# A two-layer conformer and attention trunk: the input and the parameters laid out by the host as columns, statistics and taps at other blocks

## What is computed

```python
def rms_norm(x, g):
    y = xf * lax.rsqrt(jnp.mean(xf * xf, axis=-1, keepdims=True) + RMS_EPS)
    return y.astype(x.dtype) * g

def conformer_conv(x, w_in, b_in, dw, dw_b, ln_g, ln_b, w_out, b_out):
    h = x @ w_in + b_in                 # 2048 -> 4096
    a, gate = jnp.split(h, 2, axis=-1)
    h = a * jax.nn.sigmoid(gate)
    h = causal_dwconv(h, dw, dw_b)      # 31 taps over the tokens
    h = jax.nn.silu(layer_norm(h, ln_g, ln_b))
    return h @ w_out + b_out

# in reference(): h = rms_norm(x, norm_mix[0]); x = x + conformer_conv(h, ...)
```

## Time and profile before

| what | us |
|---|---|
| median of 3 runs | 2141.56 |
| lowest and highest | 2141.47, 2142.43 |
| the profiled execution, its time | 2142.64 |
| its span, first to last instruction | 2140.8 |
| TensorE busy in it | 2125.7 |

### The profile page before, as it was taken

One profiled execution on the slowest core, in us unless ns is written; L12 is line 12 of the kernel. 1 busy time (PEld: TensorE's weight loads), 2 busy tenths in 40 slices (PEclk: granted clock), 3 DMA queues, 4 the chain that ended last, 5 costly groups with the idle time before them and its releaser, 6 DMA issues.

```text
span 2140.8 us, 30475 instructions
## 1 busy us (share of the span) xinstructions
PE 2125.7 (99%) x11011; PEld 1812.3 (85%) x11011; DVE 1452.6 (68%) x2137; ACT 1056.8 (49%) x1501; POOL 45.7 (2%) x50
## 2 busy tenths in 40 slices
PE   9999999999999999999999999999999999999998
PEld 7788788888888888888888888888888888888887
DVE  6766757777777774454688867667777777764444
ACT  7554655544445443444554444554544445444443
POOL 5300000000000000000000000000000000000000
PEclk9999999999999999999999999999999999999999
DMA  8555456666666655555656554566666666656553
GB/s 309 175 186 191 138 178 183 190 191 183 194 184 189 191 185 189 193 190 191 191 163 176 181 175 155 191 182 183 190 190 184 194 183 189 192 190 215 195 195 114
DMA packets 513820, 399.07 MB, mean 186 GB/s; under 512 B 6558, under 2 KB 425848, under 8 KB 513408
## 3 DMA queue, kind: packets, MB, share of 16 engines
q1 hardware_dynamic: 513568, 397.96, 60.0%
q10 hardware_dynamic: 192, 0.28, 0.0%
HBM read 396.11 MB, written 2.10 MB: 186 GB/s over the span
## 4 chain that ended last, share of the span: by engine, by line
PE 95%; DVE 2%; DMA 1%; ACT 1%; SPq 0%; issue 0%; DVEq 0%; ACTq 0%
PE acc L1520 35%; PE acc L1525 18%; PE acc L1554 12%; PE acc L1555 12%; PE acc L1556 12%; PE acc L1826 1%; PE acc L1825 1%; PE acc L1824 1%; DMA sb_stage<-in_conv_w_in 1%; DVE sb_w_lo L918 1%; PE aux L1595 0%; PE aux L1835 0%; ACT sb_w_hi L564 0%; PE aux L1783 0%; PE aux L1664 0%
## 5 line engine op out<-in xcount | busy, mean ns | idle before, releaser
L918 DVE TENSOR_TENSOR sb_w_lo<-sb_stage,sb_w_hi 128x1024 fp32r<-128x1024 f32 (+1 forms) x743 | 904.9, 1221 | 516.8 <-ACT sb_w_hi L564 513.4
L564 ACT ACTIVATE sb_w_hi<-sb_stage 128x1024 fp32r<-128x1024 f32 (+1 forms) x743 | 780.4, 1053 | 657.4 <-PE acc L1556 373.9
L1520 PE MATMUL acc<-sb_normed,sb_w_hi 128*128 128x512 f32 x3264 | 1027.6, 396 | 0.0
L1525 PEld LDWEIGHTS acc<-sb_normed,sb_w_lo 128*128 128x128 f32 x3264 | 613.2, 188 | 144.8
L1525 PE MATMUL acc<-sb_normed,sb_w_lo 128*128 128x256 f32 x3264 | 641.4, 278 | 0.0
L1520 PEld LDWEIGHTS acc<-sb_normed,sb_w_hi 128*128 128x128 f32 x3264 | 497.7, 189 | 0.6
L1554 PE MATMUL acc<-sb_w_hi,sb_hidden 128*128 128x512 f32 x674 | 262.5, 389 | 0.0
L1556 PE MATMUL acc<-sb_w_hi,sb_hidden 128*128 128x512 f32 x674 | 262.3, 389 | 0.0
L1555 PE MATMUL acc<-sb_w_lo,sb_hidden 128*128 128x512 f32 x674 | 262.3, 389 | 0.0
L576 ACT ACTIVATE sb_corr<-acc 128x256 f32<-128x256 f32 x204 | 76.8, 376 | 210.8 <-PE acc L1525 210.7
L1556 PEld LDWEIGHTS acc<-sb_w_hi,sb_hidden 128*128 128x128 f32 x674 | 126.5, 188 | 26.4
(11 more groups left out here) (221 smaller groups left out, 1645.1 us busy)
## 6 DMA issues: line engine op xcount, KB each, us to landing
sb_stage<-in_ffn_w_gate SPq DMA_DIRECT2D x86, 1024.0 KB, 5.4
sb_stage<-in_ffn_w_up SPq DMA_DIRECT2D x86, 1024.0 KB, 5.5
sb_stage<-in_ffn_w_down SPq DMA_DIRECT2D x80, 1024.0 KB, 5.0
sb_stage<-in_attn_w_qkv SPq DMA_DIRECT2D x48, 1024.0 KB, 5.3
sb_stage<-in_conv_w_in SPq DMA_DIRECT2D x30, 1024.0 KB, 5.6
sb_stage<-in_conv_w_out SPq DMA_DIRECT2D x16, 1024.0 KB, 5.1
sb_stage<-in_attn_w_o SPq DMA_DIRECT2D x16, 1024.0 KB, 5.0
sb_stage<-in_ffn_w_down SPq DMA_DIRECT2D x8, 768.0 KB, 4.4
```

The lines of the kernel that those rows point to most:

```text
L564: nc.scalar.activation(w_hi[:, (2 * first + h) % PIECES, 0:size], stage[:, first % STAGES, off:off + size], ACT.Copy).then_inc(hi_ready, 1)
L918: nc.vector.tensor_tensor(w_lo[:, slot, 0:size], stage[:, first % STAGES, off:off + size], w_hi[:, slot, 0:size].bitcast(F32), ALU.subtrac ...
L1520: nc.tensor.matmul(acc[:, bank, :], w_hi[:, slot, q * P:(q + 1) * P], operand[:, k, :], start=begin, stop=False, skip_group_check=True)
L1525: return nc.tensor.matmul(acc[:, bank, T:2 * T], w_lo[:, slot, q * P:(q + 1) * P], operand[:, k, 0:T], start=False, stop=end, skip_group_c ...
```

## The change

The host hands in x a second time, as columns (`x_cols`: feature on the partition, tile, token), and the parameter vectors as columns. x_cols is loaded into `x_t`, which lies over `conv` (free at that time), and ScalarE and VectorE read it in SBUF. The transposes of x, `turn_params`, its row buffers and `keep_params`' copies are gone; 13 filler matmuls (`keep_clock`) stand where 6 stood. `resid`, still needed for the squares and the residual, is loaded in two pieces of 1 MB after block 4's weights. Other steps move: the squares from turns 2 and 3 to 3 and 4, the first gate to turn 5, the row scale to turn 5, the table's split from turn 7 to 6, and in turns 4 and 5 both halves are split ahead of the small steps.

```diff
+        x_t = conv[:, :, :].rearrange("p b d -> p (b d)").rearrange("p (k t) -> p k t", t=T)
...
-                return sp.dma_start(resid[:, :, begin:end], x_in[0].rearrange("(b p) d -> p b d", p=P)[:, :, begin:end])
-            width = D // X_PARTS
-            load_x(0, 2 * P).then_inc(x_first, 16)
+                return sp.dma_start(x_t[:, begin:end, :], x_cols[:, begin:end, :])
+            width = KD // X_PARTS
+            load_x(0, 2).then_inc(x_first, 16)
...
-            sp.dma_start(rope_c[:, :], rope_rows).then_inc(rope_loaded, 16)
-            sp.dma_start(pos_i[:, :], positions[0:1, :].to_broadcast([ROT, T])).then_inc(rope_loaded, 16)
-            sp.dma_start(rows_n[:, :], norm_ffn.rearrange("l (c p) -> (l c) p", p=P)).then_inc(par_c_loaded, 16)
+            for b in range(TB):
+                sp.dma_start(resid[:, b, :], x_in[0][b * P:(b + 1) * P, :]).then_inc(resid_loaded, 16)
+            conv_in_block(STAGES + 1)
...
-            for at in range(STAGES + 1, 2 * STAGES):
+            for at in range(STAGES + 2, 2 * STAGES):
...
+            sp.dma_start(rope_c[:, :], rope_rows).then_inc(rope_loaded, 16)
+            sp.dma_start(pos_i[:, :], positions[0:1, :].to_broadcast([ROT, T])).then_inc(rope_loaded, 16)
+            sp.dma_start(par_d[:, 2 * KD:4 * KD], norm_ffn).then_inc(par_c_loaded, 16)
...
-                v = v[0].rearrange("(c p) -> c p", p=P)
-                sp.dma_start(rows_c[at:at + v.shape[0], :], v).then_inc(par_c_loaded, 16)
+                sp.dma_start(par_c[:, at:at + v.shape[1]], v).then_inc(par_c_loaded, 16)
...
-                sp.dma_start(rows_f[layer * KF:(layer + 1) * KF, 0:FTAPS, :],
-                             ffn_dw[layer].rearrange("k (c p) -> c k p", p=P)).then_inc(par_f_loaded, 16)
-                sp.dma_start(rows_f[layer * KF:(layer + 1) * KF, FTAPS, :],
-                             ffn_dw_b[layer].rearrange("(c p) -> c p", p=P)).then_inc(par_f_loaded, 16)
+                sp.dma_start(par_f[:, layer, 0:FTAPS * KF].rearrange("p (k f) -> p k f", f=KF), ffn_dw[:, layer, :, :]
+                             ).then_inc(par_f_loaded, 16)
+            sp.dma_start(par_f[:, :, FTAPS * KF:(FTAPS + 1) * KF], ffn_dw_b).then_inc(par_f_loaded, 16)
...
+                act.wait_ge(x_first if q == 0 and part[0] < 2 else x_loaded[q], 16)
...
-                    act.wait_ge(x_turned, k + 1)
-                    operand(0, normed[:, k, 0:T], aux[:, k % BANKS, 0:T], par_d[:, k:k + 1], 0)
+                    operand(0, normed[:, k, 0:T], x_t[:, k, :], par_d[:, k:k + 1], 0)
...
+                act.wait_ge(resid_loaded, 16 * TB)
...
                 act.wait_ge(dft_loaded, 16)
+                act.wait_ge(operand_ready, OPER["x"] + KD)
                 nc.scalar.activation(kern_op[:, :, :], dft_in[0:STACK, 6:8, :], ACT.Copy).then_inc(taps_high, 1)
...
-            act.wait_ge(par_kept, 1)
...
+            act.wait_ge(par_d_loaded, 16)
...
                 hi(0, (0, at + 2), 0)
-                if at in (2, 3):
-                    x_squares(2 * (at - 2))
-                    x_squares(2 * (at - 2) + 1)
-                if at == X_PARTS:
+                if at in (4, 5):
+                    hi(0, (0, at + 2), 1)
+                if at in (3, 4):
+                    x_squares(2 * (at - 3))
+                    x_squares(2 * (at - 3) + 1)
+                if at == 4:
                     taps_hi()
+                if at == 5:
                     rms_root(STAT["input"])
-                if j == 4:
+                if j == (4 if c else 5):
                     open_gate(c)
...
                         keep_conv(c - 1, b, aux)
-                if at == 7:
+                if at == 6:
                     act.wait_ge(dft_loaded, 16)
...
-                hi(0, (0, at + 2), 1)
+                if at not in (4, 5):
+                    hi(0, (0, at + 2), 1)
...
+                if at == 8:
+                    act.wait_ge(par_c_loaded, 16 * 4)
+                    act.wait_ge(par_f_loaded, 16 * 3)
...
-            def keep_params():
-                keep(1, par_c[:, :], aux[:, 1, 0:2 * KD + 2])
-                nc.vector.tensor_copy(par_d[:, 2 * KD:4 * KD], aux[:, 1, 2 * T - 2 * KD:2 * T])
-                dve.wait_ge(par_turned, 3)
-                for k in range(FTAPS + 1):
-                    ins = nc.vector.tensor_copy(par_f[:, :, k * KF:(k + 1) * KF],
-                                                aux[:, 0, k * 2 * KF:(k + 1) * 2 * KF
-                                                    ].rearrange("p (l f) -> p l f", l=2))
-                ins.then_inc(par_kept, 1)
-                dve.wait_ge(par_kept, 3)
+            def scale_subln():
+                dve.wait_ge(par_c_loaded, 16 * 4)
+                dve.wait_ge(par_f_loaded, 16 * 3)
...
                 lo(0, (0, at + 2), 0)
-                if at == X_PARTS:
+                if at in (4, 5):
+                    lo(0, (0, at + 2), 1)
+                if at == 4:
+                    taps_lo()
+                if at == 5:
                     row_squares(STAT["input"])
-                    taps_lo()
                     row_scales(STAT["input"], True)
-                if j == 4:
+                if j == (4 if c else 5):
                     keep_gate(c)
...
                         measure_conv(c - 1, b)
+                if at not in (4, 5):
+                    lo(0, (0, at + 2), 1)
                 if at == 8:
-                    keep_params()
-                lo(0, (0, at + 2), 1)
+                    scale_subln()
                 if at < 2:
...
                     nc.vector.memset(prod[:, :, :], 0.0).then_inc(prod_cleared, 1)
-                if at == 7:
+                if at == 6:
                     dve.wait_ge(dft_high, 2)
...
-            def turn_x(q, part=range(4)):
-                pe.wait_ge(x_first if q == 0 and 0 in part else x_loaded[q], 16)
-                for k in [4 * q + f for f in part]:
-                    if q:
-                        pe.wait_ge(operand_ready, OPER["x"] + k + 1 - BANKS)
-                    for b in range(TB):
-                        ins = nc.tensor.transpose(aux[:, k % BANKS, b * P:(b + 1) * P], resid[:, b, k * P:(k + 1) * P],
-                                                  ident[:, :])
-                    ins.then_inc(x_turned, 1)
...
-                    pe.wait_ge(operand_ready, OPER["x"] + KD)
...
-            def turn_params():
-                pe.wait_ge(taps_kept, 2 * CH)
-                pe.wait_ge(par_c_loaded, 16 * 4)
-                turn_rows(1, 2 * T - 2 * KD, rows_n[:, :], 2 * KD)
-                turn_rows(1, 0, rows_c[:, :], 2 * KD + 2).then_inc(par_turned, 1)
-                pe.wait_ge(par_f_loaded, 16 * 4)
-                for k in range(FTAPS + 1):
-                    ins = turn_rows(0, k * 2 * KF, rows_f[:, k, :], 2 * KF)
-                ins.then_inc(par_turned, 1)
...
-                    pe.wait_ge(par_kept, 3)
+                    pe.wait_ge(taps_kept, 2 * CH)
...
-            pe.wait_ge(par_d_loaded, 16)
-            nc.tensor.transpose(acc[:, 0, 0:2 * KD], rows_d[:, :], ident[0:2 * KD, 0:2 * KD]).then_inc(par_turned, 1)
-            turn_x(0, [0, 1])
-            keep_clock(acc[:, 3, 0:P], 6)
-            pe.wait_ge(par_kept, 1)
-            def start_x(at, k):
-                if at == 0 and k == 1:
-                    turn_x(0, [2, 3])
-                if at < X_PARTS - 1 and k == 2:
-                    turn_x(at + 1)
+            keep_clock(acc[:, 3, 0:P], 13)
...
-                elif at == 9:
-                    halfway = turn_params
...
+    def columns(v):
+        return np.ascontiguousarray(v.reshape(-1, P).T)
+    for name in ("norm_mix", "norm_ffn", "conv_ln_g", "conv_ln_b", "attn_subln_g"):
+        arrays[f"in_{name}"] = columns(inputs[name])
+    for name in ("ffn_dw", "ffn_dw_b"):
+        v = inputs[name]
+        arrays[f"in_{name}"] = columns(v).reshape(P, *v.shape[:-1], -1)
+    tokens = inputs["x"][0]
+    arrays["in_x_cols"] = np.ascontiguousarray(tokens.T.reshape(-1, P, tokens.shape[0]).transpose(1, 0, 2))
```

More of the change, by code:

```diff
@@ L125, in trunk @@
           conv_ln_g, conv_ln_b, conv_w_out, conv_b_out, attn_w_qkv, attn_lq1, attn_lk1, attn_lq2, attn_lk2,
[L126 removed]
+          attn_subln_g, attn_w_o, ffn_w_gate, ffn_w_up, ffn_dw, ffn_dw_b, ffn_w_down, rope_rows, dft_rows,
+          x_cols, out):
     _, T, D = x_in.shape
@@ L1614, in stat @@
                 ins.then_inc(stat_ready, 1)
-            def turn_rows(bank, at, src, rows):
-                return nc.tensor.transpose(aux[:, bank, at:at + rows], src, ident[0:rows, 0:rows])
             def keep_clock(out, count):
```

28 lines of the change are left out of this document (9 added, 19 removed).

## The result

The changed kernel takes **2145.34 us** in the median of 19 runs (2144.65 to 2146.42), the kernel before **2142.43 us** (2141.15 to 2143.42, 19 runs). The ratio is 1.0014, with a 95% interval of 1.0008 to 1.0020: 2.9 us slower, within the 0.2% called no change. TensorE's work shrank (busy 2123.1 us in the profile, 2125.7 before), and the time did not.

A forecast was written before the change was run, and what follows sets the result against it. TensorE, busy 2125.7 of 2140.8 us, was taken as the bound. A taps turn 1.3 us later plus 2.3 us more to `forward` gave +3.6: 2146.2 for the profiled execution, 2145.2 us as a median, range 2141.0 to 2149.5.

The forecast's parts named there:

- Block 6's landing: In the opening's load queue: block 5's weights land at 30.9 us and block 6's at 40.0, behind `resid`.
- The choice of rate: For the `resid` load in the opening: 409 GB/s as for 128 partitions elsewhere, not the taps' 276; 5.1 us.
- the second rival: In the opening, `resid` loads at the taps' 276 GB/s: block 6 at 42.5 us, total 2147.7, up to 2148.6; chance 0.25.
- The chain behind it: On ScalarE and VectorE, from block 6's weights landing to the first taps turn: 10.2 us, so the turn at 50.2.
- TensorE's arrival: TensorE reaches the first taps turn at 45.0 us, counting 3.6 saved on transposes and 1.2 lost at the start; waits 5.
- From the turn to `forward`: From the first taps turn to `forward`: 28.6 us where it was 26.3, so 2.3 us longer, set by ScalarE and VectorE.
- The waits for kept taps: In blocks 7 and 8, TensorE waits 0.8 us for the first kept taps and 2.8 us for later ones.
- a sign of being right: Waits for `keep_taps` in blocks 7 and 8 of together 3 to 4 us would show the forecast right.
- the fifth rival: TensorE's clock falls in the new 5 us wait, costing 3 us, hidden almost whole by later waits: 2145.2 to 2147; chance 0.05.
- From `forward` to the end: Behind `forward`, no new TensorE wait before the convolution's projection ends, so the 3.6 us shift reaches the end whole.
- The third rival: In the opening and behind the turn, less is lost: block 6 at 38.0 us, quicker VectorE halves; +1.0, 2142.6; chance 0.20.
- The fourth: Up to `forward`, no wait arises and the change takes its whole worth: -6.0 us, 2135.6, needing block 6 at 34.8; chance 0.05.

The follow-up runs named there:

- the first experiment: The changed kernel with 28 transposes of a constant put back on TensorE between the halves of blocks 0 to 2; 2145.4 us, 1.0016 of the kernel before.
- the second profile: The changed kernel run and profiled once more with nothing changed, on the same chip as other kernels; 2145.55 us, 1.0017 of the kernel before.
- The best kernel: The changed kernel with early taps, `resid` and bias rows behind block 6, reordered steps, 8 start fillers for 13, 13 fillers for 9 ahead of the projection; 2137.66 us.

## Why the prediction was right

**The time.** 2145.2 was forecast and 2145.34 measured. Part of that is luck: the base was 2141.56, the median of three runs, where nineteen give 2142.43, and the step was forecast at 3.6 where the medians differ by 2.9, or by 3.4 when the changed kernel was run again. The mechanism is the one forecast: a later turn, a longer stretch behind it, and the removed work in the wait.

**Block 6's landing.** Forecast 30.9 for block 5 and 40.0 for block 6; measured 30.81 and 40.29. The choice of rate was right: from 20 to 24 and 24 to 28 us, with `resid` in the queue, the changed kernel moved

```profile
DMA packets 420, 1.74 MB, mean 434 GB/s; under 512 B 29, under 2 KB 29, under 8 KB 269
```

```profile
DMA packets 484, 1.60 MB, mean 401 GB/s; under 512 B 19, under 2 KB 19, under 8 KB 378
```

so the second rival (276 GB/s) fell there. The packets of 8 KB and more in the two stretches, 151 and 106, make up the 256 rows of `resid`; the rest is weights. The row that the rate was taken from was such a mixture too, with 125 packets of 8 KB in 450. The rule of the Trainium skill ("SBUF — State Buffer", "Door 1: The DMA port swizzle") pointed the same way, and the trace agrees for 128 partitions. For the 96 partitions of the taps it agrees only in part, since shorter rows raised the stretch from 236 to 295 GB/s.

**The chain behind it.** Forecast 10.2 us, measured 50.34 - 40.29 = 10.05; the taps' low part took 2.28 instead of 2.72.

**TensorE's arrival.** Forecast 45.0, measured 50.34 - 4.66 = 45.7, with errors that cancel: the start moved by 0.02 instead of +1.2 (36 filler records in 6.26 us, 0.17 each; but with the same fillers it lies anywhere from 7.32 to 8.49 in the other profiles), the transposes were worth 2.9 instead of 3.6 (the record's 1.03 us for eight holds the tail of the last), and a wait of 1.0 ahead of block 6 was not in the sum, because with block 6 at 40.29 its first low half is ready only at 42.6 and TensorE is there a microsecond earlier. None of it matters for the end, as the first experiment shows for the transposes.

**From the turn to `forward`.** Forecast 28.6, measured 28.28, against 26.27 before. The chain on ScalarE and VectorE was as told: lambda's exponential at +13.0 for +14.2, the wait at `forward` 1.7 for 1.3. The waits for kept taps were forecast at 0.8 and 2.8 and measured at 0 and 0.6. That step left out the clock: TensorE took 7.55 us from the turn to the next one where it took 6.02 before, and used up 1.5 us of these waits. With fillers in the long wait they were 1.9 together, still short of the 3 to 4 us named as a sign of being right, since lambda's exponential and the kept taps behind it came about 1.1 us sooner than forecast. So the fifth rival's first half came true in the forecast's own case, at 1.5 us, and 2.3 in the second profile, of the 3 that it was given, and hidden as it said. That the granted clock would fall had a chance of 0.05 and no term in the sum; that the sum held in spite of it is a matter of the waits behind, and in part luck. "TensorE: Matmul & The Clock Gate", section "What's actually happening", in the Trainium skill has an idle TensorE fall to 1.2 GHz, and the granted clock of 0.55 and 0.59 behind the wait agrees.

**From `forward` to the end.** It was said that the shift reaches the end whole. It does in structure: `forward` is 3.47 us later, and so is the next wait, at 211.50 for 208.05. The run with the taps in short rows shows that a late load there can swallow 0.8 us of such a shift. In the profiled executions the spans differ by 2.5 only, since the kernel before lost 1.0 us to a fall of the clock behind 222 us, which is told below.

**The third rival** (less is lost) had block 6 at 38.0, which did not come. **The fourth** (the whole worth) needed 34.8: with `resid` late the landing was 35.4, and even then TensorE waited 3.3 us for kept taps, which that rival did not count. The best kernel came to -4.4 us of the -6.0.

## What to carry to other kernels

An engine that waits gains nothing from doing less: ask what the wait hangs on, and move that first. Here 3.6 us of work came off TensorE (2.9 of transposes and 0.7 of `turn_params`), and the price was a second copy of the input in the load queue and steps moved behind the wait; the order in which ScalarE and VectorE take their steps, ahead of or behind a transfer that they wait for, was worth as much as the whole change. A step that needs no late transfer belongs into the wait for it.
